# Second mixer: odd token tiles kept in opposite order of 8-token blocks, so that two token tiles share one stationary operand

## The chip, the core and the metric

The kernel runs on one core of a Trainium2 chip. The time is that of one execution on the device, in microseconds (us). The kernel before takes 2377.02 us, the median of three runs (2376.27 to 2377.44). It is written engine by engine: each of the five engines (TensorE, VectorE, ScalarE, GpSimd and SyncE, which issues most DMAs) works through its own list in order, and semaphores order them among each other.

## The reference

Four layers over 512 tokens of width 1024, in fp32, each a mixer and a feed-forward network. The change is in the second mixer, a gated recurrence with 8 heads of width 128. For each head:

```python
f = lb + (1.0 - lb) * jax.nn.sigmoid(f_logit)      # forget gate, per token and key channel
k = 1.0 - f
b = cumsum(log(f))                                 # along the tokens
o_inter = einsum('bhtk,bhkv->bhtv', q_t * exp(b_t), state)
decay = exp(where(causal, b_t - b_s, -inf))        # t: query token, s: key token
scores = einsum('bhtk,bhsk,bhtsk->bhts', q_t, k_t, decay)
o = o_inter + einsum('bhts,bhsv->bhtv', scores, v_t)
new_state = exp(b_last)[..., None] * state + einsum('bhsk,bhsv->bhkv', k_t * exp(b_last - b_t), v_t)
# then rmsnorm(o, g_norm_w) * silu(g), and a projection with w_out
```

## The kernel before

The 512 tokens are four tiles of 128. The recurrence is computed with a state for each tile, and the scores within a tile need exp(b_t - b_s) for each pair of tokens. That factor can't be split into a query and a key factor over the whole tile without overflow, so the tile is cut in four **levels** and a rest. Level 0 takes queries of the second 64 tokens against keys of the first 64; level 1 does the same within each block of 64 (32 against 32), level 2 within 32, level 3 within 16; **near** is what is left, inside blocks of 8. At level l the middle value of b in each block is subtracted from both sides: queries get exp(b - middle), keys exp(middle - b).

The tile `lv[l]` (128 channels by 512 tokens) holds, at level l, key factors in the first half of each block and query factors in the second. GpSimd writes the exponents (L1984 queries, L1985 keys, 256 columns each, for levels 1 to 3; level 0 is done by ScalarE from b itself, L1668 and L1673). ScalarE takes exp in place (`ex`, L1646), VectorE multiplies with q and k (L1848, and L1822 in the helper `tt_`). TensorE then multiplies, for each token tile, the whole 128 columns of `lv[l]` as the stationary operand with the 64 query columns as the moving one (`level`, L1521): 4 matmuls a level, 16 a head, of 128 by 64 results. All of them are fp32, and each appears in the profile as two passes. VectorE's `take` (L1836) copies the valid parts of the results into the score tile under a mask, ScalarE does it for level 0 (`taken`). Near has its own tiles `near_q` and `near_k` and 128 columns for both (L1530).

The loop runs in **rounds** p = 0 to 10, and each engine has its own order of a round. In round p head p is projected (two units of weights: q, then the forget logits), head m = p-1 has its levels, head b = p-2 its near products, state and output, head o = p-3 its norm. What closes the round is a chain over all engines:

- TensorE ends the second unit of head p (bank 1). VectorE reads it (L1939, writes `sq`), ScalarE makes four activations of it, VectorE makes k (L1947) and the scan that gives b (L1952; its semaphore is `hg_b`).
- With b, GpSimd runs through levels 1, 2, 3 (semaphore `hg_d` after each) and then near (L1988), which waits until TensorE has read the old `near_q`. ScalarE runs through level 0, level 1, the state's query factor, a weight conversion, levels 2 and 3 (waiting on `hg_d`), the copy of q out of bank 0, then `factor_log` (L1679: reads the norm's sum from bank 4), exp, the copy `keys`, near and the decayed keys.
- TensorE, meanwhile, does levels 0 and 1 of head m, the output of head b, levels 2 and 3, the first unit of the next round, `norm`, `near` and `turn`. `turn` (L1498, four transposes into bank 4) waits for `hg_rstd`, that is for ScalarE's `factor_log`, which reads the same bank. Behind it stand the second unit of that round and the state products.

Heads 0 to 7 get their b at 720.92, 736.02, 753.09, 771.60, 790.36, 809.33, 828.41 and 847.50 us. I call "+x" a time x us after the b of a head. After the last head TensorE fills the remaining waits with parts of the output projection (`part`).

## Time and profile before

| | us |
|---|---|
| median of three runs | 2377.02 |
| profiled execution | 2377.56 |
| its span, first to last instruction | 2375.8 |
| TensorE busy | 2364.9 (100%) |
| VectorE busy | 1326.7 (56%) |
| ScalarE busy | 1031.4 (43%) |
| GpSimd busy | 62.4 (3%) |
| chain of waits | TensorE 95%, VectorE 3%, ScalarE 2% |

Between the span and the profiled execution's time lie 1.8 us, outside of all instructions. The profile names engines PE (TensorE), PEld (its weight loads), DVE (VectorE), ACT (ScalarE), POOL (GpSimd) and SP. A matmul's duration holds its way through the array, so matmuls overlap: the time that a group costs is its busy time over its count, not its mean duration. The heads of the second mixer lie between 716 and 883 us.

### The profile page before, as it was taken

The page shows a single profiled execution, that of the slowest core. Times are in us where ns is not written, and L with a number is a line of the kernel's source. Part 1 is how long each engine was busy: PE and PEld are TensorE (multiplying, and loading weights), DVE is VectorE, ACT ScalarE, POOL GpSimd, SP SyncE. Part 2 cuts the span into 40 slices and gives each one's busy share as a digit, 9 for nine tenths or more (in the row PEclk, how much of TensorE's full clock was granted, in tenths as well). Part 3 has the DMA queues.
Part 4 walks back from the last instruction along what each step waited for, and adds up shares of the span by engine and source line. Part 5 has one row for each costly group of instructions (what it writes and reads, how often), then busy time and mean ns, then how long its engine had stood idle before and what let it go on. Part 6 is the DMA issues. An engine that isn't in the chain of part 4 may idle for free.

```text
span 2375.8 us, 30572 instructions
## 1 busy us (share of the span) xinstructions
PE 2364.9 (100%) x11344; PEld 1946.5 (82%) x11344; DVE 1326.7 (56%) x1950; ACT 1031.4 (43%) x1655; POOL 62.4 (3%) x100
## 2 busy tenths in 40 slices
PE   9999999999999999999999999999999999999999
PEld 7777888888888888888888778888888878888887
DVE  6765744432637867444325776777533556677731
ACT  5555522222447855222324664444322545444420
POOL 1000000000002310000000000000001000000000
PEclk9999999999999999999999999999999999999999
DMA  4112222332221113323322113232323222222332
GB/s 159 54 63 80 89 89 90 105 122 91 81 98 63 54 54 98 97 88 101 116 94 89 63 45 116 89 103 92 107 97 107 80 71 96 92 96 95 104 98 83
DMA packets 69332, 214.30 MB, mean 90 GB/s; under 512 B 7280, under 2 KB 18544, under 8 KB 69232
## 3 DMA queue, kind: packets, MB, share of 16 engines
q1 hardware_dynamic: 67696, 210.72, 26.8%
q0 software_dynamic: 1536, 2.21, 0.3%
q8 instruction: 67, 1.10, 0.2%
q14 instruction: 33, 0.27, 0.0%
HBM read 210.80 MB, written 2.10 MB: 90 GB/s over the span
## 4 chain that ended last, share of the span: by engine, by line
PE 95%; DVE 3%; ACT 2%; issue 0%; DMA 0%; SPq 0%; DVEq 0%; ACTq 0%
PE bank L264 26%; PE bank L266 26%; PE bank L265 26%; PE bank L387 5%; PE bank L379 4%; PE bank L1134 1%; PE bank L1521 1%; PE bank L1125 1%; PE bank L1171 1%; PE bank L2061 0%; DVE w_lo L238 0%; DMA raw<-in_w_fox_v 0%; PE bank L2509 0%; PE bank L2497 0%; DVE h L612 0%
## 5 line engine op out<-in xcount | busy, mean ns | idle before, releaser
L264 PE MATMUL bank<-x_hi,w_hi 128*128 128x512 f32 x1792 | 706.9, 394 | 0.1
L266 PE MATMUL bank<-x_hi,w_lo 128*128 128x512 f32 x1792 | 698.5, 390 | 0.0
L265 PE MATMUL bank<-x_lo,w_hi 128*128 128x512 f32 x1792 | 698.3, 390 | 0.0
L238 DVE TENSOR_TENSOR w_lo<-raw,w_hi 128x1024 fp32r<-128x1024 f32 (+1 forms) x367 | 470.4, 1291 | 239.8 <-ACT w_hi L233 239.0
L233 ACT ACTIVATE w_hi<-raw 128x1024 fp32r<-128x1024 f32 (+1 forms) x367 | 403.7, 1109 | 170.7 <-PE bank L266 102.7
L264 PEld LDWEIGHTS bank<-x_hi,w_hi 128*128 128x128 f32 x1792 | 336.7, 188 | 74.1 <-issue 4.2
L266 PEld LDWEIGHTS bank<-x_hi,w_lo 128*128 128x128 f32 x1792 | 336.8, 188 | 70.9
L265 PEld LDWEIGHTS bank<-x_lo,w_hi 128*128 128x128 f32 x1792 | 336.8, 188 | 70.3 <-issue 1.9
L920 DVE TENSOR_TENSOR bank<-bank,rstd 128x512 f32<-128x512 f32 x176 | 122.6, 699 | 292.9 <-PE bank L266 291.8
L264 PE MATMUL bank<-up_a_hi,w_hi 128*128 128x512 f32 (+1 forms) x748 | 282.0, 377 | 0.0
L266 PE MATMUL bank<-up_a_hi,w_lo 128*128 128x512 f32 (+1 forms) x748 | 281.6, 377 | 0.0
L265 PE MATMUL bank<-up_a_lo,w_hi 128*128 128x512 f32 (+1 forms) x748 | 281.6, 377 | 0.0
L264 PEld LDWEIGHTS bank<-up_a_hi,w_hi 128*128 128x128 f32 x748 | 140.7, 188 | 25.9
L265 PEld LDWEIGHTS bank<-up_a_lo,w_hi 128*128 128x128 f32 x748 | 140.7, 188 | 25.8
L266 PEld LDWEIGHTS bank<-up_a_hi,w_lo 128*128 128x128 f32 x748 | 140.7, 188 | 25.7
L886 ACT ACTIVATE up_a_hi<-gated 128x512 f32 (+1 forms) x88 | 55.6, 632 | 222.4 <-DVE gated L956 222.1
L734 DVE TENSOR_TENSOR h<-h,bank 128x512 f32<-128x512 f32 x32 | 22.0, 686 | 152.0 <-PE bank L266 152.0
L264 PE MATMUL bank<-mix_hi,w_hi 128*128 128x512 f32 (+1 forms) x272 | 106.1, 390 | 0.5 <-ACT y L720 0.5
L266 PE MATMUL bank<-mix_hi,w_lo 128*128 128x512 f32 (+1 forms) x272 | 102.6, 377 | 0.0
L265 PE MATMUL bank<-mix_lo,w_hi 128*128 128x512 f32 (+1 forms) x272 | 102.6, 377 | 0.0
L877 ACT ACTIVATE up_conv_g<-bank,cols 128x512 f32<-128x512 f32 x44 | 34.3, 779 | 139.7 <-DVE bank L920 139.7
L379 PE MATMUL bank<-w_hi,x_hi 128*128 128x512 f32 x224 | 88.7, 398 | 1.4 <-DVE x_lo L504 1.2
(361 smaller groups left out, 2714.8 us busy)
## 6 DMA issues: line engine op xcount, KB each, us to landing
raw<-in_w_up SPq DMA_DIRECT2D x176, 512.0 KB, 3.3
raw<-in_w_down SPq DMA_DIRECT2D x64, 704.0 KB, 4.4
raw<-in_w_fox_qk SPq DMA_DIRECT2D x16, 512.0 KB, 3.3
raw<-in_w_hgrn_qf SPq DMA_DIRECT2D x16, 512.0 KB, 3.3
raw<-in_w_fox_out SPq DMA_DIRECT2D x8, 512.0 KB, 3.2
raw<-in_w_hgrn_v SPq DMA_DIRECT2D x8, 512.0 KB, 3.4
raw<-in_w_hgrn_g SPq DMA_DIRECT2D x8, 512.0 KB, 3.2
raw<-in_w_hgrn_out SPq DMA_DIRECT2D x8, 512.0 KB, 3.3
```

Source lines behind the costliest of these rows:

```text
L233: nc.scalar.activation(w_hi[:, slot, 0:size], raw[:, slot % 2, 0:size], ACT.Copy).then_inc(sem("hi_ready"), 1)
L238: nc.vector.tensor_tensor(w_lo[:, slot, 0:size], raw[:, slot % 2, 0:size], w_hi[:, slot, 0:size].bitcast(F32), ALU.subtract).then_inc(sem( ...
L264: nc.tensor.matmul(out, w[0], x[0], start=first, stop=False)
L265: nc.tensor.matmul(out, w[0], x[1], start=False, stop=False)
L266: return nc.tensor.matmul(out, w[1], x[0], start=False, stop=last)
L379: return nc.tensor.matmul(ps[bank + tt][:].rearrange("p (n x) -> p n x", n=2), (x_hi, x_lo)[x_part][:, k, tt * P:(tt + 1) * P], w, start=f ...
L387: return nc.tensor.matmul(ps[bank + n][:, half], (w_hi, w_lo)[w_part][:, k // 2, at:at + P], (x_hi, x_lo)[x_part][:, k, half], start=first ...
L877: nc.scalar.activation(buf, ps[up_bank(j, 2 * p + half)][:], ACT.Identity, bias=cols[:, bass.ds(cb + 6 * FT + idx, 1)], scale=cols[:, bass ...
L886: nc.scalar.activation(a_hi[:, ft, :], gated[:, p, :], ACT.Copy).then_inc(sem("ahi_ready"), 1)
L920: nc.vector.tensor_tensor(bank[:], bank[:], rstd[:], ALU.mult).then_inc(sem("scaled"), 1)
L1125: ins = nc.tensor.transpose(ps[bank][:, at:at + P], prob[:, src:src + P], ident[:])
L1134: ins = nc.tensor.matmul(ps[bank][r, kt * P:T], v[:, kt, r], pt[hd][:, PT_AT[kt]:PT_AT[kt] + n], start=kt == 0, stop=kt == TT - 1)
```

## The change

Each `lv[l]` now holds keys in its left 256 columns (`lv_k`) and queries in its right 256 (`lv_q`), without gaps. The token tiles are taken in pairs (0, 1) and (2, 3). The even tile of a pair keeps its order, and its keys lie in the first halves of the blocks; the odd tile's blocks of 8 tokens are kept in opposite order, so that its keys lie in the second halves. So 128 columns hold the 64 keys of both tiles. One matmul has these as stationary operand and the 64 queries of each of the two tiles, 128 columns, as moving one.

What follows from that layout: `hk`, `near_k` and `kd_flat` hold even tiles first, then the odd ones with their blocks reversed; the masks are built for even and odd tiles; the value tiles of odd token tiles are written to `hv_odd` (in the place that `hq` and `hk` take later) and moved into `hv` by 16 DMAs with their 8-row blocks reversed; TensorE waits for these (`hg_turned`) before the heads.

```diff
+        hv_odd = nc.alloc_sbuf_tensor_at("hgrn_v_odd", [P, 8, 2, P], F32, offset=hg.at)
-        hk = [hg.take(f"k_{x}", [P, T]) for x in "ab"]
+        hk = [hg.take(f"k_{x}", [P, 2, 2, P]) for x in "ab"]
+        lv_k, lv_q = [t[:, 0:T // 2] for t in lv], [t[:, T // 2:T] for t in lv]
...
+        def in_order(t, odd):
+            return eights(t)[:, :, ::-1, :] if odd else eights(t)
...
+            wait(pe, "hg_turned", 16 * 16)
             def level(m, l):
...
-                for tt in range(TT):
-                    t = lv[l][:, tt * P:(tt + 1) * P]
-                    at = 256 * (l % 2) + 64 * tt
-                    out = ps[2 + l // 2][:, at:at + 64].rearrange("p (g y) -> p g y", y=64 >> l)
-                    ins = nc.tensor.matmul(out, t, halves(t, l)[:, :, 1, :], start=True, stop=True)
+                for u in range(2):
+                    sl = slice(u * P, (u + 1) * P)
+                    at = 256 * (l % 2) + P * u
+                    ins = nc.tensor.matmul(ps[2 + l // 2][:, at:at + P], lv_k[l][:, sl], lv_q[l][:, sl], start=True, stop=True)
...
+                            to = lv_k[0][:, P * (tt // 2) + 64 * (tt % 2):P * (tt // 2) + 64 * (tt % 2) + 64]
+                            nc.scalar.activation(row(to, tt % 2), row(hb[:, tt * P:mid + 1], 0), ACT.Exp,
...
-                        ex(near_k[:], near_q[:], "hg_e", -1.0)
+                        for odd in range(2):
+                            ins = nc.scalar.activation(in_order(near_k[:, odd], odd), eights(parity(near_q[:], odd)), ACT.Exp, scale=-1.0)
+                        ins.then_inc(sem("hg_e"), 1)
...
-                        cp(halves(scs[m % 2][:], 0)[0:64, :, 1, :], ps[2][0:64, 0:256].rearrange("p (g y) -> p g y", y=64),
-                           "hg_take0")
+                        for odd in range(2):
+                            r = ROWS[odd]
+                            ins = nc.scalar.activation(parity(scs[m % 2][:], odd)[r, :, 64:P],
+                                                       ps[2][r, 0:256].rearrange("p (u o y) -> p u o y", u=2, o=2)[:, :, odd, :], ACT.Copy)
+                        ins.then_inc(sem("hg_take0"), 1)
...
-            dve.wait_ge(sem("hg_consts"), 32)
+            dve.wait_ge(sem("hg_consts"), 16 * 18)
+            wait(dve, "hg_masks", 8)
...
-                        t = halves(lv[l][:], l)
-                        nc.vector.tensor_tensor(t[:, :, 1, :], halves(hq[m % 2][:], l)[:, :, 1, :], t[:, :, 1, :], ALU.mult)
-                        tt_(t[:, :, 0, :], halves(hk[m % 2][:], l)[:, :, 0, :], t[:, :, 0, :], ALU.mult, "hg_pr")
+                        q = packed(lv_q[l], l)
+                        nc.vector.tensor_tensor(q, halves(hq[m % 2][:], l)[:, :, 1, :], q, ALU.mult)
+                        k = lv_k[l].rearrange("p (g x y) -> p g x y", x=2, y=64 >> l)
+                        tt_(k, keys_of(hk[m % 2], l), k, ALU.mult, "hg_pr")
...
-                    nc.vector.tensor_scalar(hk[p % 2][:], sg1, lbt[:, 8, p:p + 1], lbt[:, 7, p:p + 1],
-                                            ALU.mult, ALU.add).then_inc(sem("hg_k"), 1)
+                    for odd in range(2):
+                        ins = nc.vector.tensor_scalar(in_order(hk[p % 2][:, odd], odd), eights(parity(sg1, odd)), lbt[:, 8, p:p + 1],
+                                                      lbt[:, 7, p:p + 1], ALU.mult, ALU.add)
+                    ins.then_inc(sem("hg_k"), 1)
...
+            for a in range(0, P, 8):
+                nc.gpsimd.dma_start(raw_masks[1][P - 8 - a:P - a], io["lv_mask"][a:a + 8]).then_inc(sem("hg_consts"), 16)
             nc.gpsimd.dma_start(scan_mask[:], io["scan_mask"]).then_inc(sem("hg_consts"), 16)
+            wait(pool, "hg_consts", 16 * 18)
+            pool.wait_ge(sem("tokens_out"), 16)
+            for a in range(0, P, 8):
+                to = hv[P - 8 - a:P - a].rearrange("p m (u o) c -> p (m u) o c", o=2)[:, :, 1, :]
+                nc.gpsimd.dma_start(to, hv_odd[a:a + 8].rearrange("p m u c -> p (m u) c")).then_inc(sem("hg_turned"), 16)
...
-                    nc.gpsimd.tensor_tensor(d_[:, :, 1, :], b_[:, :, 1, :], middle, ALU.subtract)
-                    nc.gpsimd.tensor_tensor(d_[:, :, 0, :], middle, b_[:, :, 0, :], ALU.subtract).then_inc(sem("hg_d"), 1)
+                    nc.gpsimd.tensor_tensor(packed(lv_q[l], l), b_[:, :, 1, :], middle, ALU.subtract)
+                    even = hb[:].rearrange("p (u o g x y) -> p u o g x y", u=2, o=2, x=2, y=half)[:, :, 0, :, 0, :]
+                    nc.gpsimd.tensor_tensor(by_role(lv_k[l], l)[:, :, :, 0, :],
+                                            even[:, :, :, half - 1:half].to_broadcast([P, 2, 64 // half, half]), even, ALU.subtract)
+                    for u in range(2):
+                        odd = halves(hb[:, P * (2 * u + 1):P * (2 * u + 2)], l)[:, :, 0, :]
+                        to = eights(halves(lv_k[l][:, P * u:P * (u + 1)], l)[:, :, 1, :])[:, ::-1, ::-1, :]
+                        ins = nc.gpsimd.tensor_tensor(to, eights(odd[:, :, half - 1:half].to_broadcast([P, 64 // half, half])),
+                                                      eights(odd), ALU.subtract)
+                    ins.then_inc(sem("hg_d"), 1)
```

TensorE, the levels and the output of one round, first before, then changed (line numbers are each kernel's own; `hgrn_lv_108` to `111` before and `109` to `112` after are the tiles of levels 0 to 3):

```order
L1521 MATMUL bank<-hgrn_lv_108 128x64 x4
L1521 MATMUL bank<-hgrn_lv_109 128x64 x4
L1557 MATMUL bank<-hgrn_scores_b,hgrn_v 128x128 x2
L1559 MATMUL bank<-hgrn_qe_b,hgrn_st 128x128
...
L1521 MATMUL bank<-hgrn_lv_110 128x64 x4
L1521 MATMUL bank<-hgrn_lv_111 128x64 x4
```

```order
L1557 MATMUL bank<-hgrn_lv_109 128x128 x2
L1557 MATMUL bank<-hgrn_lv_110 128x128 x2
L1595 MATMUL bank<-hgrn_scores_b,hgrn_v 128x128 x2
L1597 MATMUL bank<-hgrn_qe_b,hgrn_st 128x128
...
L1557 MATMUL bank<-hgrn_lv_111 128x128 x2
L1557 MATMUL bank<-hgrn_lv_112 128x128 x2
```

Nothing has moved; each level is two matmuls of 128 columns where it was four of 64.

GpSimd, one head, before and changed (`hgrn_b` is the scan's result, the tiles of levels 1 to 3 are `109` to `111` before and `110` to `112` after):

```order
L1984 TENSOR_TENSOR hgrn_lv_109<-hgrn_b 128x8x32
L1985 TENSOR_TENSOR hgrn_lv_109<-hgrn_b 128x8x32
L1984 TENSOR_TENSOR hgrn_lv_110<-hgrn_b 128x16x16
L1985 TENSOR_TENSOR hgrn_lv_110<-hgrn_b 128x16x16
L1984 TENSOR_TENSOR hgrn_lv_111<-hgrn_b 128x32x8
L1985 TENSOR_TENSOR hgrn_lv_111<-hgrn_b 128x32x8
L1988 TENSOR_TENSOR hgrn_near_q<-hgrn_b 128x512
```

```order
L2049 TENSOR_TENSOR hgrn_lv_110<-hgrn_b 128x4x32
L2054 TENSOR_TENSOR hgrn_lv_110<-hgrn_b 128x2x4x8 x2
L2047 TENSOR_TENSOR hgrn_lv_111<-hgrn_b 128x256
L2049 TENSOR_TENSOR hgrn_lv_111<-hgrn_b 128x8x16
L2054 TENSOR_TENSOR hgrn_lv_111<-hgrn_b 128x4x2x8 x2
L2047 TENSOR_TENSOR hgrn_lv_112<-hgrn_b 128x256
L2049 TENSOR_TENSOR hgrn_lv_112<-hgrn_b 128x16x8
L2054 TENSOR_TENSOR hgrn_lv_112<-hgrn_b 128x8x8 x2
L2059 TENSOR_TENSOR hgrn_near_q<-hgrn_b 128x512
```

The queries' instruction stays (L2047, of 256 columns; that of the first level stands just above the piece), and the keys' one of 256 has become three: one of 128 columns and two of 64. A head has 12 level instructions on GpSimd where it had 6.

## Rows read from the trace of the kernel before

**Rows 1.** Busy time by engine, heads 3 to 6 (stretch, us, then engines, PEclk, DMA)
```profile
771.60:847.50 75.90, 75.90 (x456) 65.83 (x455) 61.99 (x108) 60.56 (x132) 20.48 (x29) 1.00 0.17 56
```

**Rows 2.** TensorE's levels among its groups: shape, count | busy us, mean ns | idle
```profile
L1521 PE MATMUL bank<-hgrn_lv 128*128 128x64 f32 x256 | 30.4, 272 | 0.0
```

**Rows 3.** Chain of waits, round of head 6 (start us, us, what)
```profile
823.51 1.73 PE bank L1521 x16
...
834.99 0.89 PE bank L1530 x8
835.88 0.51 PE bank L1498 x4
...
842.60 1.73 PE bank L1521 x16
```

**Rows 4.** TensorE's waits, whole program
```profile
PE bank L1498 <- ACT hgrn_hr L1679: 1.9, 1, 1.9
```

**Rows 5.** Chain of waits, turn of head 1 and what follows
```profile
757.88 0.63 PE bank L1498 x4
...
766.27 1.73 PE bank L1521 x16
```

**Rows 6.** Busy time, TensorE's clock just behind that wait
```profile
760.00:761.00 1.00, 1.00 (x3) 0.72 (x3) 1.00 (x2) 0.97 (x3) 0.00 (x0) 0.50 0.00 0
```

**Rows 7.** GpSimd in order of time (start us, us, instruction)
```profile
616.04 0.58 POOL L1976 DMA_DIRECT2D hgrn_lv_mask<-in_lv_mask  x1 [607.01 <-PE bank L266]
...
720.92 0.63 POOL L1984 TENSOR_TENSOR hgrn_lv<-hgrn_b 128x256 f32<-128x256 f32 x1 [103.77 <-DVE hgrn_b L1952]
...
771.60 0.63 POOL L1984 TENSOR_TENSOR hgrn_lv<-hgrn_b 128x256 f32<-128x256 f32 x1 [13.38 <-DVE hgrn_b L1952]
...
828.41 0.64 POOL L1984 TENSOR_TENSOR hgrn_lv<-hgrn_b 128x256 f32<-128x256 f32 x1 [10.49 <-DVE hgrn_b L1952]
...
830.76 0.86 POOL L1984 TENSOR_TENSOR hgrn_lv<-hgrn_b 128x256 f32<-128x256 f32 x1
831.58 0.80 POOL L1985 TENSOR_TENSOR hgrn_lv<-hgrn_b 128x256 f32<-128x256 f32 x1
835.97 1.04 POOL L1988 TENSOR_TENSOR hgrn_near_q<-hgrn_b 128x512 f32<-128x512 f32 x1 [3.59 <-PE bank L1530]
847.50 0.63 POOL L1984 TENSOR_TENSOR hgrn_lv<-hgrn_b 128x256 f32<-128x256 f32 x1 [10.49 <-DVE hgrn_b L1952]
```

**Rows 8.** VectorE in order of time, head 6 and the last head
```profile
823.55 0.69 DVE L1939 TENSOR_SCALAR sq<-bank 128x512 f32<-128x512 f32 x1 [0.20 <-PE bank L266]
...
830.62 0.46 DVE L1848 TENSOR_TENSOR hgrn_lv<-hgrn_q_a,hgrn_lv 128x256 f32<-128x256 f32 x1 [1.07 <-ACT hgrn_lv L1673]
831.00 0.90 DVE L1822 TENSOR_TENSOR hgrn_lv<-hgrn_k_a,hgrn_lv 128x256 f32<-128x256 f32 x1
...
832.58 0.41 DVE L1822 TENSOR_TENSOR hgrn_lv<-hgrn_k_a,hgrn_lv 128x256 f32<-128x256 f32 x1
...
838.37 0.69 DVE L1822 TENSOR_TENSOR hgrn_near_k<-hgrn_k_a,hgrn_near_k 128x512 f32<-128x512 f32 x1 [1.01 <-ACT hgrn_near_q L1646]
...
842.63 0.69 DVE L1939 TENSOR_SCALAR sq<-bank 128x512 f32<-128x512 f32 x1 [0.20 <-PE bank L266]
...
859.99 0.69 DVE L1822 TENSOR_TENSOR hgrn_near_q<-hgrn_q_b,hgrn_near_q 128x512 f32<-128x512 f32 x1
```

**Rows 9.** TensorE in order of time, the last head's near products
```profile
862.47 1.06 PE L1530 MATMUL bank<-hgrn_near_q,hgrn_near_k 128*128 128x128 f32 x8
```

**Rows 10.** ScalarE in order of time, head 6
```profile
832.48 1.14 ACT L1646 ACTIVATE hgrn_lv<-hgrn_lv 128x512 f32<-128x512 f32 x2
...
835.03 0.60 ACT L1679 ACTIVATE hgrn_hr<-bank 128x512 f32<-128x512 f32 x1 [0.26 <-PE bank L1566]
```

**Rows 11.** ScalarE in order of time, entry: last value tiles
```profile
662.96 2.41 ACT L583 ACTIVATE hgrn_v<-bank,cols 128x512 f32<-128x512 f32 x4
```

**Rows 12.** VectorE in order of time, before the heads
```profile
702.48 0.06 DVE L1818 MEMSET hgrn_scan_mask<- 128x4 f32 x1
```

More of the change, by code:

```diff
@@ L1479, in build @@
         st = hg.take("st", [P, TT - 1, P])
-        lv_mask = hg.take("lv_mask", [P, 4, P], U32)
+        lv_mask = [hg.take(f"lv_mask{l}", [P, T // 2], U32) for l in range(1, LEVELS)]
+        near_mask = hg.take("near_mask", [P, 2, P], U32)
         scan_mask = hg.take("scan_mask", [P, T])
@@ L1529, in near @@
                     sl = slice(tt * P, (tt + 1) * P)
-                    ins = nc.tensor.matmul(ps[6][:, sl], near_k[:, sl], near_q[:, sl], start=True, stop=True)
+                    ins = nc.tensor.matmul(ps[6][:, sl], near_k[:, tt % 2, tt // 2, :], near_q[:, sl], start=True, stop=True)
                 ins.then_inc(sem("hg_lv"), 1)
@@ L1637, in act_hgrn @@
         def act_hgrn(act):
[L1639 removed]
+            act_enter(act, 2, lambda b, tt: hv_odd[:, 4 * b:4 * b + 4, tt // 2, :] if tt % 2 else hv[:, 4 * b:4 * b + 4, tt, :])
             act.wait_ge(sem("hg_lb"), 1)
@@ L1730, in decayed @@
                             last = (tt + 1) * P - 1
-                            ins = nc.scalar.activation(kd_flat[:, sl], hb[:, sl], ACT.Exp, bias=hb[:, last:last + 1], scale=-1.0)
+                            to = kd_flat[:, tt % 2, tt // 2, :]
+                            ins = nc.scalar.activation(row(to, tt % 2), row(hb[:, sl], 0), ACT.Exp, bias=hb[:, last:last + 1],
+                                                       scale=-1.0)
                         ins.then_inc(sem("hg_e"), 1)
```

53 lines of the change are left out of this document (38 added, 15 removed).

## The prediction

> **What bounds the kernel now.** I read the page first: TensorE is busy for the whole span. The busy time by stretch then shows that this holds in the changed stage as well, from head 3 to head 7: 75.90 of 75.90 us [rows 1]. So time that TensorE is spared there is time gained, as long as nothing else stands right behind it. But VectorE (61.99) and ScalarE (60.56) are busy for four fifths of the same stretch [rows 1], in one chain with each other, and the question is how much slack they have.
>
> The chain of waits gives a round: levels at 823.51, the same at 842.60, so 19.09 us [rows 3]. GpSimd's first instruction of a head marks when b is there: heads 0, 3, 6 and 7 at 720.92, 771.60, 828.41 and 847.50 [rows 7]. The last round took 19.09 us and the four from head 3 on 75.90 together, while the three before took 50.68. In those first rounds VectorE sets the pace, TensorE runs ahead and is idle once, 1.9 us at the turn that waits for ScalarE [rows 4]. That wait is the place to watch: in round 6 ScalarE's log (L1679) ends at 835.63 [rows 10] and the turn starts at 835.88 [rows 3]. The slack is a semaphore's way long.
>
> **What TensorE saves.** Its level group is 256 passes, busy 30.4 us [rows 2], part of it overlap at the ends; the chain has 16 of them in 1.73 us, 108 ns each [rows 3]. The nearest row for 128 columns is near: 8 passes in 0.89 us, 111 ns each [rows 3]. So the columns are nearly free and the passes cost. The change makes 16 passes of a head's 32: 32 x 108 - 16 x 111 = 3.46 - 1.78 = 1.7 us a head, 13.5 us in all. If the wider matmul cost twice as much, it would be nothing; the near row speaks against that. A round of TensorE's work falls from 19.09 to 17.4.
>
> **What the other engines pay in a round.** Per level GpSimd has one instruction of 256 columns, one of 128 and two of 64 in place of two of 256. A 256 one takes 0.64 alone and a 512 one 1.04 [rows 7]: 1.6 ns a column and 0.2 fixed, from start to start about 0.6, 0.37 and 0.27 for 256, 128 and 64. A level takes 1.5 instead of 1.2, three levels 1.0 more. That is an estimate by extrapolation, and blocks that are walked backwards are in no row. Bounds: nothing (if an instruction costs by its columns alone) and 2.5 us a head (if a backward one of 64 costs as much as one of 128 and a little more). I take 1.0.
>
> There is a second cost, since GpSimd and VectorE hinder each other. VectorE's product with 256 columns takes 0.41 when GpSimd is idle (832.58) and 0.90 at 831.00; the latter ends 0.28 after GpSimd's instruction of 830.76 does (831.62), and GpSimd's next one, started at 831.58, needs 0.80 for what takes 0.6 [rows 7, 8]. So each waits for the other's running instruction, one by one in turn. I lay out the new head by that. GpSimd is at level 2's keys when VectorE starts its products at +2.2 (830.62 [rows 8]), and has seven level instructions left where it had three. They alternate with VectorE's products: the last key instruction of level 3 ends at about +5.9, in place of +3.97 (832.38) [rows 7].
>
> ScalarE takes up levels 2 and 3 at +4.07 and needs 1.14 for both [rows 10]. Level 3 would start at +6.0, not +4.6, and end at +6.6. The copy of q and the log follow, 0.5 apart and 0.6 long as the log's row shows: log done at +7.7. The turn starts at +7.8, and from the turn to the next round's levels TensorE needs 842.60 - 835.88 = 6.72 us [rows 3]: +14.5. VectorE reads bank 1 at once (0.03 after the levels' row, 842.63), b follows 828.41 - 823.55 = 4.86 later [rows 7, 8], and the split of k in two adds 0.1 (fixed part of one more instruction). That closes the round at **19.6 us**.
>
> VectorE's own chain gives the same. From its first product (830.62) to bank 1 (842.63) lie 12.0 us, with 1.0 of idle time ahead of 838.37, 0.2 ahead of bank 1, and about 1.0 lost to GpSimd [rows 8]. The rest is 9.8. Now near_q's exponents come earlier as TensorE is faster, and GpSimd's instruction of 1.04 [rows 7] then meets VectorE's conversion instead of its reads of PSUM; the loss becomes some 2.7. So 4.86 + 2.2 + 9.8 + 2.7 = 19.6. Two chains of equal length make the number firmer.
>
> **What the wait does to the clock.** TensorE's work of 17.4 in a round of 19.6 leaves a wait of 2.2 us at each turn. The one wait of that size in the trace, 1.9 us ahead of the turn at 757.88, is followed by a stretch at a granted clock of 0.50, the 1.2 GHz level [rows 4, 6]; from that turn to the next levels it took 766.27 - 757.88 = 8.39 us where round 6 took 6.72 [rows 3, 5]. So such a wait costs 1.67 more, and it lies in the chain that closes the round. A round with it takes 21.3. Bounds: in no round and in each; I take it in 6 of 10, 1.0 us a round.
>
> **The sum**, against the profiled execution (2377.56; the median is 0.5 below):
> - Heads 0 to 3: VectorE sets the pace, and what TensorE saves is idle time. VectorE loses 0.6 more to GpSimd and 0.1 in k: 3 x 0.7 = +2.1. Bounds 0 and +6.
> - Heads 3 to 7: 4 x (19.6 + 1.0) - 75.90 = +6.5. Bounds: 4 x 18.4 - 75.90 = -2.3 (no loss to GpSimd's longer list) and 4 x 21.3 - 75.90 = +9.3.
> - Behind head 7's b: the levels of heads 6 and 7 are 3.4 us shorter, and TensorE has parts of the output projection to fill with. But the last head's products are not far ahead: near_q is there at 860.68 for a matmul at 862.47 [rows 8, 9], 1.8 us. ScalarE's start into that head comes earlier with TensorE's norm, which gives some of it back. I take -2.2, bounds -3.4 and 0.
> - ScalarE's near in two instructions and `taken` in two: 0.2 each (the fixed part). Taken lies in ScalarE's wait for b; near stands in front of VectorE's near products, which are as late for VectorE's own sake. Nothing, or 0.2 a round.
> - The turning of the values: the last value tiles are written at 665.4 [rows 11], 16 issues of 0.58 [rows 7] end at 675 and 14 small copies at about 680. VectorE gets to its wait at 702 [rows 12], TensorE later still. Hidden, with more than 20 us to go; if it weren't, each us late is one lost. The 17 mask DMAs go out from 616 on and have longer.
>
> 2.1 + 6.5 - 2.2 = +6.4: 2384.0, or 2383.5 on the scale of the median.
>
> The Trainium skill has a price for GpSimd's small instructions ("GPSIMD Engine Reference", section 3.1, Elementwise): about 2.6 cycles an element for two inputs, at 1.2 GHz. Set against the 0.6 us of a 256-column one it leaves almost no fixed part, a level would grow by an estimated 0.1 us instead of 0.3, level 3 would come before +5.3, and the round would end near 19.0 us, as long as today's; the slope between this trace's rows of 256 and 512 columns is 1.6 ns, not 2.2, so the trace doesn't agree, and no row shows 64 columns. It would bring the time toward the second rival below.
>
> **Rivals.**
> - TensorE stays the bound and gets all of it: -13.5, so 2363.5. For it: it is busy without a gap now [rows 1]. Against it: the log reaches the turn with 0.25 us to spare, and the chain over VectorE can't close in 17.4. Chance 0.05.
> - Faster, by one mechanism: GpSimd's split instructions cost by columns alone, so level 3's exponents are at hand when ScalarE comes for them. The round is then 4.86 to b, +5.2 end of level 3, +6.4 log, +6.5 turn, +13.2 bank 1: with VectorE's own length about 18.4. Heads 3 to 7 give -2.3, the tail -2.2, the first heads nothing: 2372.5. It decides at the point where level 3's `hg_d` comes before +4.6. Chance 0.10.
> - The round is 19.6, but a wait of 2.2 us leaves the clock alone (one example is thin): 2.1 + 2.5 - 2.2 = +2.4, 2379.5. Chance 0.22.
> - Backward blocks are slow on GpSimd, 0.2 more for each of six instructions: 1.2 us more in each of seven rounds, +8 on top: 2391.5. For it: no row shows them. Chance 0.13.
> - The forecast, 2383.5, with its own range of 2380 to 2388: chance 0.50.
>
> About 0.2%, 4.8 us, is what a measurement of this kernel can tell from no change. Faster by that: the first rival and half of the second, 0.11. Within: the third, the rest of the second and a fifth of the forecast, 0.34. Slower: 0.55. The range goes from the second rival to the fourth, 2372 to 2392.
>
> **What would show it.** Right: L1557's passes number 128 at about 111 ns; TensorE waits at nearly each turn for ScalarE's log, some 2 us; the busy time by stretch has a granted clock of 0.5 for some 3 us behind more than half of these waits; b is 20 to 21 us apart from head 3 on; GpSimd's 64-column instructions take 0.3. Wrong: turns without waits and rounds below 19 us (then level 3's exponents came in time), waits without a fall of the clock, or a wait on `hg_turned` or the masks before the heads.

## The result, and the profile after

| | before | changed |
|---|---|---|
| median, us (9 runs each) | 2377.4 (2376.27 to 2379.15) | 2384.62 (2382.88 to 2386.37) |
| profiled execution; span | 2377.56; 2375.8 | 2383.5; 2381.7 |
| TensorE, GpSimd busy | 2364.9, 62.4 | 2355.5, 98.0 |
| b of heads 0, 3, 7 at | 720.92, 771.60, 847.50 | 720.92, 771.97, 852.41 |

The changed kernel is slower: ratio 1.0029, 95% interval 1.0021 to 1.0038. Of the 5.9 us between the two profiled executions 0.4 arise in heads 0 to 3, 4.5 in heads 3 to 7, and 1.0 behind head 7's b.

TensorE saved what it should. The group of its levels, from the costliest groups of the changed kernel (busy us, mean ns of one | idle time ahead, and what ended it), answers to [rows 2]: half the passes, 17.4 us busy where it was 30.4.

```profile
L1557 PE MATMUL bank<-hgrn_lv 128*128 128x128 f32 x128 | 17.4, 277 | 2.0 <-DVE hgrn_lv L1869 2.0
```

And it lost more than that in waits: its busy time fell by 9.4 us in all and the span grew by 5.9, so it is idle for 15.3 us more. Its two largest waits over the whole program (us, times, longest); before, the one at the turn was 1.9 us [rows 4]:

```profile
PE bank L1575 <- ACT hgrn_hr L1718: 11.3, 6, 2.8
PE bank L1595 <- DVE hgrn_st L1944: 2.8, 4, 1.1
```

The busy time by stretch (us, then PE, PEld, DVE, ACT, POOL busy, PEclk, DMA) answers to [rows 1] and [rows 6]. From head 3 to head 7 TensorE is busy for 70.58 of 80.44 us; the rest it waits. The three single microseconds lie behind three turns that waited, and only the last two stand at a granted clock of 0.50:

```profile
771.97:852.41 80.44, 70.58 (x383) 59.40 (x382) 67.09 (x113) 61.14 (x140) 27.97 (x52) 0.96 0.16 53
781.00:782.00 1.00, 1.00 (x6) 0.83 (x5) 1.00 (x2) 0.97 (x3) 0.00 (x0) 1.00 0.76 188
...
820.00:821.00 1.00, 1.00 (x4) 0.81 (x3) 0.86 (x3) 0.97 (x4) 0.00 (x0) 0.50 0.67 254
840.00:841.00 1.00, 1.00 (x4) 0.80 (x3) 1.00 (x3) 0.97 (x3) 0.00 (x0) 0.50 0.38 74
```

Five turns waited for 1.9 us or more. Four of them follow in TensorE's order of time; the fifth is at 798.89, with 1.91. Behind 757.97, 779.56 and 798.89 the clock stayed at 1.00, behind 818.21 and 839.10 it fell to half for 3 to 4 us, after a shorter wait than the first two:

```profile
757.97 0.63 PE L1575 MATMUL bank<-ident,hgrn_kd_flat 128*128 128x128 f32 x4 [2.21 <-ACT hgrn_hr L1718]
...
779.56 0.63 PE L1575 MATMUL bank<-ident,hgrn_kd_flat 128*128 128x128 f32 x4 [2.78 <-ACT hgrn_hr L1718]
...
818.21 0.63 PE L1575 MATMUL bank<-ident,hgrn_kd_flat 128*128 128x128 f32 x4 [1.92 <-ACT hgrn_hr L1718]
...
839.10 0.63 PE L1575 MATMUL bank<-ident,hgrn_kd_flat 128*128 128x128 f32 x4 [1.91 <-ACT hgrn_hr L1718]
```

What the turn waits for starts on GpSimd. Its order of time answers to [rows 7]; head 4 stands for all. The 64-column instructions are two of 0.27 from start to start when it is alone (792.25) and 0.6 each when VectorE is at its products (795.94); level 3 ends at 797.11, 5.8 us behind b:

```profile
771.97 0.63 POOL L2047 TENSOR_TENSOR hgrn_lv<-hgrn_b 128x256 f32<-128x256 f32 x1 [11.79 <-DVE hgrn_b L2000]
...
791.30 0.63 POOL L2047 TENSOR_TENSOR hgrn_lv<-hgrn_b 128x256 f32<-128x256 f32 x1 [12.34 <-DVE hgrn_b L2000]
791.89 0.40 POOL L2049 TENSOR_TENSOR hgrn_lv<-hgrn_b 128x128 f32<-128x128 f32 x1
792.25 0.54 POOL L2054 TENSOR_TENSOR hgrn_lv<-hgrn_b 128x64 f32<-128x64 f32 x2
...
795.94 1.17 POOL L2054 TENSOR_TENSOR hgrn_lv<-hgrn_b 128x64 f32<-128x64 f32 x2
797.07 1.22 POOL L2059 TENSOR_TENSOR hgrn_near_q<-hgrn_b 128x512 f32<-128x512 f32 x1
810.61 0.64 POOL L2047 TENSOR_TENSOR hgrn_lv<-hgrn_b 128x256 f32<-128x256 f32 x1 [12.32 <-DVE hgrn_b L2000]
...
831.50 0.63 POOL L2047 TENSOR_TENSOR hgrn_lv<-hgrn_b 128x256 f32<-128x256 f32 x1 [13.89 <-DVE hgrn_b L2000]
...
852.41 0.63 POOL L2047 TENSOR_TENSOR hgrn_lv<-hgrn_b 128x256 f32<-128x256 f32 x1 [13.91 <-DVE hgrn_b L2000]
```

ScalarE's level 3 waits 1.16 us for it and the log comes after, for [rows 10]:

```profile
797.14 0.63 ACT L1684 ACTIVATE hgrn_lv<-hgrn_lv 128x512 f32<-128x512 f32 x1 [1.16 <-POOL hgrn_lv L2054]
...
798.16 0.59 ACT L1718 ACTIVATE hgrn_hr<-bank 128x512 f32<-128x512 f32 x1
```

VectorE in the same head, for [rows 8]: products of 0.51 and 0.89, a conversion of 2.06 us (near_q's exponents at 797.07 lie across it; before it took 1.22), and the clamp of the logits (the read of bank 1) 12.2 us behind the first product. The last product ends with the copy under the near mask at 799.96:

```profile
793.51 0.53 DVE L1893 TENSOR_TENSOR hgrn_lv<-hgrn_q_a,hgrn_lv 128x256 f32<-128x256 f32 x1 [1.48 <-ACT hgrn_lv L1712]
...
794.83 0.89 DVE L1869 TENSOR_TENSOR hgrn_lv<-hgrn_k_a,hgrn_lv 128x256 f32<-128x256 f32 x1
...
797.31 2.06 DVE L238 TENSOR_TENSOR w_lo<-raw,w_hi 128x1024 fp32r<-128x1024 f32 x1
...
799.96 0.74 DVE L1878 COPY_PREDICATED hgrn_scores_b<-hgrn_near_mask,bank 128x512 f32<-128x512 uint32 x1
...
805.74 0.69 DVE L1985 TENSOR_SCALAR sq<-bank 128x512 f32<-128x512 f32 x1 [0.22 <-PE bank L266]
```

Behind head 7's b the chain of waits no longer runs along TensorE, as it did before, but through VectorE's list for the last head (start us, us, what):

```profile
867.95 1.22 DVE w_lo L238
...
872.60 0.70 DVE hgrn_ho L1869
...
874.92 0.36 DVE hgrn_st L1944
...
879.09 0.86 PE bank L1604 x2
```

The last norm's first matmul starts at 878.92 where before it was 873.52.

### The profile page after: what moved, and what is told of

Read it like the earlier page. It is cut to its first block, busy times and chain, and to the rows that moved or that the text cites. A ratio compares the mean times of both kernels' runs of the same rounds, so it can differ in the third digit from the quotient of the medians.

```text
span 2381.7 us, 30437 instructions
## 1 busy us (share of the span) xinstructions
PE 2355.5 (99%) x11216; PEld 1934.6 (81%) x11216; DVE 1334.0 (56%) x1958; ACT 1034.5 (43%) x1671; POOL 98.0 (4%) x194
## 4 chain that ended last, share of the span: by engine, by line
PE 89%; DVE 5%; ACT 3%; POOL 1%; issue 1%; DMA 1%; DVEq 0%; ACTq 0%; SPq 0%
PE bank L264 25%; PE bank L266 25%; PE bank L265 25%; PE bank L387 5%; PE bank L379 4%; PE bank L1134 1%; PE bank L1125 1%; PE bank L1171 1%; DVE w_lo L238 1%; PE bank L2132 0%; ACT sq L1684 0%; POOL hgrn_lv L2054 0%; DVE hgrn_b L2000 0%; DMA raw<-in_w_up 0%; POOL hgrn_lv L2047 0%
## 5 line engine op out<-in xcount | busy, mean ns | idle before, releaser
L238 DVE TENSOR_TENSOR w_lo<-raw,w_hi 128x1024 fp32r<-128x1024 f32 (+1 forms) x367 | 476.3, 1307 | 239.4 <-ACT w_hi L233 238.5
L264 PEld LDWEIGHTS bank<-up_a_hi,w_hi 128*128 128x128 f32 x748 | 140.7, 188 | 25.8
L266 PEld LDWEIGHTS bank<-up_a_hi,w_lo 128*128 128x128 f32 x748 | 140.7, 188 | 25.6
L877 ACT ACTIVATE up_conv_g<-bank,cols 128x512 f32<-128x512 f32 x44 | 34.3, 779 | 139.7 <-DVE bank L920 139.7
```

Source lines behind the costliest of these rows:

```text
L238: nc.vector.tensor_tensor(w_lo[:, slot, 0:size], raw[:, slot % 2, 0:size], w_hi[:, slot, 0:size].bitcast(F32), ALU.subtract).then_inc(sem( ...
L264: nc.tensor.matmul(out, w[0], x[0], start=first, stop=False)
L266: return nc.tensor.matmul(out, w[1], x[0], start=False, stop=last)
L877: nc.scalar.activation(buf, ps[up_bank(j, 2 * p + half)][:], ACT.Identity, bias=cols[:, bass.ds(cb + 6 * FT + idx, 1)], scale=cols[:, bass ...
```

## The experiments

Twelve kernels, each timed against the kernel before on the same chip. The times of the kernel before were 2377.60 to 2377.66 in each set. A round is the distance of b from head 3 to head 7 over four; the waits are TensorE's at the turns; the last column counts the turns and norms with a wait of 1.88 us or more, and how many of them had a stretch at half clock behind them. All but the times are read from one profile each. The letters (T, A to G, L) name the theories and rivals of the expectation that is printed with each experiment. The 95% intervals are some 2 us wide to either side; where two experiments differ by less, the reading rests on the rounds of the profiles, which repeat from head to head, and not on the medians.

| kernel | us | ratio (95%) | b 0, 3, 7 | round | waits at turns | half clock |
|---|---|---|---|---|---|---|
| before | 2377.6 | 1 | 720.92, 771.60, 847.50 | 18.98 | 1.9 | 1 of 1 |
| changed | 2384.62 | 1.0029 (1.0021–1.0038) | 720.92, 771.97, 852.41 | 20.11 | 11.3 | 2 of 5 |
| 1 TensorE's part alone | 2375.37 | 0.999 (0.9981–0.9999) | 720.87, 771.16, 845.30 | 18.54 | 6.9 | 1 of 1 |
| 2 all but TensorE's part | 2380.36 | 1.0013 (1.0004–1.0022) | 721.30, 772.48, 849.77 | 19.32 | 3.8 | 0 of 2 |
| 3 GpSimd's list short | 2375.69 | 0.9991 (0.9982–1.0) | 720.54, 770.83, 844.98 | 18.54 | 7.2 | 1 of 1 |
| 4 filled waits | 2379.86 | 1.0009 (1.0–1.0018) | 720.56, 771.66, 848.75 | 19.27 | 1.8 | none |
| 5 log first | 2377.81 | 1.0001 (0.9992–1.001) | 720.59, 771.65, 846.74 | 18.77 | 6.8 | 0 of 2 |
| 6 b turned once | 2378.95 | 1.0006 (0.9997–1.0015) | 721.16, 772.68, 848.50 | 18.96 | 8.8 | 0 of 2 |
| 7 both | 2378.89 | 1.0006 (0.9997–1.0015) | 720.55, 772.06, 847.91 | 18.96 | 6.5 | 1 of 2 |
| 8 both, first state on ScalarE | 2377.39 | 0.9999 (0.999–1.0008) | 720.49, 771.67, 846.15 | 18.62 | 6.5 | 1 of 2 |
| 9 log first, first state on ScalarE | 2376.36 | 0.9994 (0.9985–1.0003) | 721.65, 772.38, 846.17 | 18.45 | 6.2 | 1 of 2 |
| 10 the same, low half on GpSimd | 2373.32 | 0.9982 (0.9973–0.9991) | 721.03, 771.15, 842.73 | 17.90 | 4.6 | 0 of 1 |
| 11 kernel before, with the edits of 9 | 2376.8 | 0.9999 (0.999–1.0008) | 721.21, 771.55, 846.34 | 18.70 | 1.9 | 0 of 1 |
| 12 one more GpSimd instruction | 2383.97 | 1.0027 (1.0017–1.0037) | 721.04, 774.61, 853.12 | 19.63 | 6.7 | 1 of 2 |

**1. TensorE's part alone**, in the kernel before:

```diff
-                for tt in range(TT):
-                    t = lv[l][:, tt * P:(tt + 1) * P]
-                    at = 256 * (l % 2) + 64 * tt
+                for u in range(2):
+                    t = lv[l][:, 2 * u * P:(2 * u + 1) * P]
+                    at = 256 * (l % 2) + P * u
...
+                    two = lv[l][:, 2 * u * P:(2 * u + 2) * P]
+                    ins = nc.tensor.matmul(out, t, halves(two, l)[:, :, 1, :], start=True, stop=True)
```

> The kernel before, in which TensorE alone is changed: each level is two matmuls of 128 columns (the key operand of an even token tile for both tiles of the pair) in place of four of 64. GpSimd, ScalarE and VectorE run their old lists; the scores of the odd tiles come out wrong. Theory T (what TensorE saves turns into waits because the round over VectorE, GpSimd, ScalarE's log and the turn is nearly as long): b comes every 18.4 to 18.8 us from head 3 on instead of 19.0, TensorE waits 1 to 1.5 us at the turns for ScalarE's log, total 2372 to 2376, so at most a third of the 13.5 us that the passes save. Rival A (TensorE is the bound and the loss in the changed kernel comes from the other engines' longer lists alone): rounds of 17.4, total 2363.5. Rival B (128-column passes bring nothing): 2377.

Measured 2375.37, rounds of 18.54: theory T. Of 13.5 us on TensorE 2.3 reach the end; the rest stands in its waits (6.9 us at the turns, where it was 1.9).

It also isolates the tail: b of head 7 comes 2.2 us sooner than before and the profiled execution ends 2.3 sooner, so behind head 7 the shorter levels bring nothing, or 0.1.

**2. All but TensorE's part:** the changed kernel with four matmuls of 64 columns a level.

```diff
-                for u in range(2):
-                    sl = slice(u * P, (u + 1) * P)
+                for tt in range(TT):
+                    keys = lv_k[l][:, (tt // 2) * P:(tt // 2 + 1) * P]
...
+                    ins = nc.tensor.matmul(ps[2 + l // 2][:, at:at + 64], keys, lv_q[l][:, 64 * tt:64 * tt + 64], start=True, stop=True)
```

> The changed kernel, in which TensorE still takes four matmuls of 64 columns a level (the shared key operand is loaded for each tile); everything else as in the changed kernel. Theory T: the round is closed by the other engines, so TensorE's extra 1.7 us a head fall into its waits: rounds of 19.3 with waits at the turns of 0.2 to 0.5 us and the granted clock never at half behind them, except early; total 2381 to 2385, the same as the changed kernel or up to 3 us faster because the two rounds at half clock go. Rival A (TensorE's time counts): 1.7 us a head more, 2384.6 + 8 or more = 2392 to 2398.

Measured 2380.36, rounds of 19.32 as in the undisturbed ones of the changed kernel (19.33 and 19.31). TensorE has 1.7 us a head more to do and the kernel is 4.3 us faster than the changed one, more than T's 3 (the time is 0.6 under T's range): of the changed kernel's waits the last three before the tail are gone (798.89, 818.21 and 839.10), and with them the stretches at half clock. Two are left:

```profile
PE bank L1575 <- ACT hgrn_hr L1718: 3.8, 2, 1.9
```

**3. GpSimd's list short:**

```diff
-                    nc.gpsimd.tensor_tensor(by_role(lv_k[l], l)[:, :, :, 0, :],
...
-                    for u in range(2):
...
+                    nc.gpsimd.tensor_tensor(packed(lv_k[l], l), middle, b_[:, :, 0, :], ALU.subtract).then_inc(sem("hg_d"), 1)
```

> The changed kernel, in which GpSimd writes a level's key exponents with one instruction of 256 columns, in natural order, where the changed kernel has one of 128 and two of 64 (the scores of the odd tiles come out wrong). Theory T (GpSimd's longer list makes level 3 late and holds VectorE up): level 3's exponents come at +4.0 to +4.3 after b instead of +5.8, ScalarE doesn't wait for them, rounds 18.4 to 18.8, total 2372 to 2376. Rival C (the loss is from the turning, the split instructions of ScalarE and VectorE, or the clock): 2382 to 2385, rounds unchanged at 19.3 and more.

Measured 2375.69 and 18.54: T, and within 0.3 us of experiment 1, which has none of the other edits. So the turning of values and masks, the two-part instructions of ScalarE and VectorE and the reversed blocks there cost nothing that shows; GpSimd's list makes the whole 0.78 us a round (19.32 against 18.54). GpSimd ends level 3 at 830.39, 3.95 behind b, and VectorE has no idle time between its first product and the clamp, 11.5 us later (GpSimd, then VectorE, in order of time):

```profile
829.60 0.79 POOL L2048 TENSOR_TENSOR hgrn_lv<-hgrn_b 128x256 f32<-128x256 f32 x1
831.70 1.15 POOL L2051 TENSOR_TENSOR hgrn_near_q<-hgrn_b 128x512 f32<-128x512 f32 x1 [1.30 <-PE bank L1566]
```

```profile
828.65 0.46 DVE L1893 TENSOR_TENSOR hgrn_lv<-hgrn_q_a,hgrn_lv 128x256 f32<-128x256 f32 x1 [1.48 <-ACT hgrn_lv L1712]
...
840.13 0.69 DVE L1985 TENSOR_SCALAR sq<-bank 128x512 f32<-128x512 f32 x1
```

**4. Filled waits:**

```diff
                 wait(pe, "hg_kdh", m)
+                if 1 <= m <= 5:
+                    wait(pe, "hg_st", 3 * m)
+                    for _ in range(8):
+                        nc.tensor.matmul(ps[5][:, 0:P], ones[:], ident[:], start=True, stop=True)
                 wait(pe, "hg_rstd", 2 * norms - 1)
```

> The changed kernel with eight extra TensorE matmuls of 128 columns (constants into a bank that is free then) ahead of the wait for ScalarE's log at the turns of heads 1 to 5, so that TensorE is busy for about 1.8 us where it waited 1.9 to 2.8. Theory D (a part of the loss is the clock: two rounds of 20.9 among those of 19.3): no stretch at half clock from head 3 on, all rounds 19.3, total 2381 to 2382, 3 us under the changed kernel. Rival E (the longer rounds have another cause and the clock follows): 2384.6 as the changed kernel. If the eight matmuls take more than the wait: 2386 to 2390.

Measured 2379.86, rounds of 19.27, no stretch at half clock: theory D, with 4.8 us back where 3 were expected (its range began at 2381). Between the two profiled executions it is 4.2, of which 3.4 from head 3 to head 7, two stretches of 1.6 and a little. The rest may lie in the choice of the profiled execution. The changed kernel's nine executions had mean granted clocks of 0.997 to 0.999, three of each: those at 0.999 (the profiled one among them) took 2383.6 on average, those at 0.998 2384.2, those at 0.997 2385.3. The filled kernel's had 1.000 each and lie within 0.8 us. So by and large the executions with more time at half clock are the longer ones. The waits for the log are down to 1.8 us, the longest to 0.9.

**5. Log first,** in the changed kernel, on ScalarE:

```diff
-                        if o:
+                        if o and p >= HEADS:
                             factor_log()
...
                     level(2)
-                    level(3)
                     used(act, u0 + 2 * p)
                     wait(act, "hg_qe", p - 1)
                     cp(hq[p % 2][:], ps[0][:], "hg_q")
+                    if norm and o:
+                        factor_log()
+                    level(3)
                     factor()
```

> The changed kernel with ScalarE's order altered in heads 1 to 4 and on: behind level 2's exponents it takes the copy of q and the norm's log first and level 3's exponents after them, so the turn no longer waits behind GpSimd's list. Two theories of what closes the 19.3 us round. Theory F (two chains of equal length, the log's over TensorE and VectorE's own list with what it loses to GpSimd): the turns come 1 us or more sooner, VectorE loses its 0.2 and 0.1 us of idle time, rounds of 18.9 to 19.1, no stretch at half clock from head 3 on, total 2378.5 to 2381. Theory G (the log's chain alone closes it, VectorE only follows): rounds of 17.8 to 18.3, total 2372 to 2376.

Measured 2377.81, rounds of 18.77: neither range, but near F's (0.1 us a round and 0.7 in the time under it) and 0.5 a round above G's. The turn comes sooner, with 1.02 us of waiting, and VectorE has no idle time from its first product to the clamp, 11.7 us in place of 12.2 (VectorE, then TensorE):

```profile
811.40 0.53 DVE L1895 TENSOR_TENSOR hgrn_lv<-hgrn_q_b,hgrn_lv 128x256 f32<-128x256 f32 x1 [1.48 <-ACT hgrn_lv L1712]
...
815.21 2.06 DVE L238 TENSOR_TENSOR w_lo<-raw,w_hi 128x1024 fp32r<-128x1024 f32 x1
817.19 0.41 DVE L1895 TENSOR_TENSOR hgrn_lv<-hgrn_q_b,hgrn_lv 128x256 f32<-128x256 f32 x1
...
817.86 0.72 DVE L1880 COPY_PREDICATED hgrn_scores_a<-hgrn_near_mask,bank 128x512 f32<-128x512 uint32 x1
...
823.10 0.69 DVE L1987 TENSOR_SCALAR sq<-bank 128x512 f32<-128x512 f32 x1
```

```profile
814.99 0.63 PE L1575 MATMUL bank<-ident,hgrn_kd_flat 128*128 128x128 f32 x4 [1.02 <-ACT hgrn_hr L1718]
```

So the log's chain closed the changed kernel's round, and VectorE's list stood 0.55 us behind it. Of the 0.78 us a round that GpSimd's longer list costs (experiment 3), 0.55 went through level 3, the log and the turn; 0.23 (18.77 against 18.54) is what it takes from VectorE.

**6. b turned once:** VectorE copies b behind the scan, and GpSimd needs two instructions of 256 columns a level.

```diff
+                    wait(pool, "hg_bt", m + 1)
+                    k = lv_k[l].rearrange("p (g x y) -> p g x y", x=2, y=half)
+                    nc.gpsimd.tensor_tensor(k, middles_of(hbt, l), keys_of(hbt, l), ALU.subtract).then_inc(sem("hg_d"), 1)
...
+                    for odd in range(2):
+                        ins = nc.vector.tensor_copy(in_order(hbt[:, odd], odd), eights(parity(hb[:], odd)))
```

> The changed kernel with full output: VectorE copies b once per head behind the scan, odd tiles in the opposite order of blocks, and GpSimd then needs one instruction of 256 columns for a level's keys instead of 128 + 64 + 64. VectorE has 1.5 us of idle time behind the scan for the two copies (some 0.7 us). Theory T (GpSimd's list is what costs): level 3's exponents at +4.3 to +4.8, rounds of 18.5 to 18.8, total 2374.5 to 2377, under the kernel before by 1 to 3 us. Rival (the copies wait for GpSimd's lock and push the first products or level 1 back by 0.5 us): rounds of 19.0, 2378 to 2379.

Measured 2378.95, rounds of 18.96: the rival, though level 3's exponents are there at +4.4, as T had it. The two engines meet at the copy, GpSimd's first key instruction starts at +0.97 where it was +0.6, and VectorE's first three products (0.87, 0.89 and 0.83) each meet one of GpSimd's instructions; the product of the queries takes 1.55 us, since near_q's exponents lie across it (GpSimd, then VectorE):

```profile
829.54 0.74 POOL L2058 TENSOR_TENSOR hgrn_lv<-hgrn_b 128x256 f32<-128x256 f32 x1 [12.46 <-DVE hgrn_b L2007]
830.51 0.62 POOL L2061 TENSOR_TENSOR hgrn_lv<-hgrn_b_turned 128x256 f32<-128x256 f32 x1 [0.23 <-DVE hgrn_b_turned L2010]
```

```profile
831.75 0.87 DVE L1900 TENSOR_TENSOR hgrn_lv<-hgrn_q_a,hgrn_lv 128x256 f32<-128x256 f32 x1 [0.50 <-ACT hgrn_lv L1719]
...
834.44 1.55 DVE L1876 TENSOR_TENSOR hgrn_qe_a<-hgrn_q_a,hgrn_qe_a 128x512 f32<-128x512 f32 x1
```

**7. Both edits.**

> The two edits together: b copied in turned order for GpSimd, and ScalarE's log ahead of level 3. Theory F (VectorE's list closes the round once GpSimd's is short: no idle time on it from the first product to the clamp of the logits): rounds of 18.4 to 18.6 as without the log's edit, total 2373.5 to 2376.5, with TensorE's waits moved from the turn to the norm or the levels. Theory G (the log at the turn closes it): rounds of 17.4 to 17.8, total 2368 to 2371.

Measured 2378.89, rounds of 18.96, the same as 6 to 0.01 us, though TensorE's waits at the turns fell from 8.8 to 6.5 us. Both ranges were missed. G is out by 1.2 us a round: the log at the turn isn't the bound once VectorE's list is longer. F's mechanism may stand, but its figures were too low, since they rested on those expected for experiment 6.

**8. The first state on ScalarE,** added to 7:

```diff
+                def first_state():
+                    wait(act, "hg_ds", b + 1)
+                    wait(act, "hg_o", b)
+                    cp(st[:, 0, :], ps[5][:, 0:P], "hg_st")
...
-                        nc.vector.tensor_copy(st[:, 0, :], ps[5][:, 0:P]).then_inc(sem("hg_st"), 1)
+                        if not (proj and b > 0):
+                            nc.vector.tensor_copy(st[:, 0, :], ps[5][:, 0:P]).then_inc(sem("hg_st"), 1)
```

> The same two edits and a third: ScalarE, idle there for 1.6 us, makes the first state copy of heads 1 to 5 (128 columns from PSUM, 0.29 to 0.33 us on VectorE) in VectorE's place. Theory F (VectorE's list is the bound): each round 0.3 shorter than with the two edits, 18.1 to 18.3, total 1.0 to 2.0 us less than with the two. Theory G or any other bound (TensorE, ScalarE): no difference.

Measured 2377.39: 1.5 us less than 7, the round 0.34 less, for an instruction of 0.3 on VectorE. That is F, on its mechanism; the absolute 18.1 to 18.3 missed with 7.

**9. The same edit on experiment 5.**

> The changed kernel with two edits of ScalarE's order, and nothing on GpSimd: the norm's log ahead of level 3 (18.78 us a round, 2377.8, alone), and the first state copy of heads 1 to 5 on ScalarE in VectorE's place. Theory F (VectorE's list, without idle time from the first product to the clamp, closes the round): the copy's 0.30 to 0.33 us comes off each round, 18.45 us, total 2375.3 to 2376.3, under the kernel before. Rival (another engine is as long by now): 18.7 and more, 2377.2 to 2378.

Measured 2376.36 and 18.45. F, at the edge: the round is as expected to 0.01, the time 0.1 above the range.

**10. The low half on GpSimd,** added to 9:

```diff
+                if 0 <= m - 2 < HEADS - 3:
+                    wait(pool, "hg_outh", m - 1)
+                    nc.gpsimd.tensor_tensor(mix_lo[:, m - 2, :], ho, mix_hi[:, m - 2, :].bitcast(F32),
+                                            ALU.subtract).then_inc(sem("hg_out"), 1)
```

> As the kernel above, and GpSimd, idle for 10 us of each round, subtracts the low half of the mixed output (512 columns) for heads 0 to 4 in VectorE's place. VectorE's instruction is 0.60 us long, GpSimd's 1.04, and VectorE's neighbours there that read PSUM (the states, the clamp) don't collide with it. Theory F with collisions: between nothing and 0.4 us less a round, 18.05 to 18.45, total 2373 to 2376. If the whole of GpSimd's instruction falls on VectorE's SBUF-only instructions: 0.4 us more a round, 2378.

Measured 2373.32, 11.3 us under the changed kernel and 4.3 under the one before; its interval doesn't reach 1. The round fell by 0.55, to 17.90, which is nearly all of VectorE's 0.60 and 0.15 more than the most that was expected. GpSimd's instruction lies beside VectorE's states and clamp, which read PSUM, and these keep their 0.73 and 0.69 (GpSimd, then VectorE):

```profile
819.43 1.28 POOL L2073 TENSOR_TENSOR mix_lo<-hgrn_ho,mix_hi 128x512 fp32r<-128x512 f32 x1 [5.58 <-ACT mix_hi L1687]
```

```profile
819.20 0.73 DVE L1954 SCALAR_TENSOR_TENSOR hgrn_st<-hgrn_st,hgrn_dec_a,bank 128x128 f32<-128x128 f32 x2
820.01 0.69 DVE L1995 TENSOR_SCALAR sq<-bank 128x512 f32<-128x512 f32 x1
```

**11. The edits of 9 on the kernel before.**

> The kernel before with the same two edits of ScalarE's order (the log ahead of level 3, the first state copy on ScalarE). Theory T (the kernel before is bound by TensorE from head 3 on, the changed one by VectorE): rounds of 19.0 to 19.09 as before, total 2375.5 to 2377.6 (the only gain at head 1's turn, whose wait and clock cost at most 2 us). Rival (VectorE or the log bound the kernel before too): rounds of 18.7, 2374 or less.

Measured 2376.8: within T's range, no difference from before. The mean round is the rival's, though: 18.19 and 18.41 at first, then 19.11 and 19.08. VectorE still set the pace in those first rounds, which T had not said; relieved, it seems to let TensorE use up its lead, until TensorE is the bound again (GpSimd's first instruction of heads 4 to 6):

```profile
789.74 0.63 POOL L1994 TENSOR_TENSOR hgrn_lv<-hgrn_b 128x256 f32<-128x256 f32 x1 [10.32 <-DVE hgrn_b L1962]
...
808.15 0.63 POOL L1994 TENSOR_TENSOR hgrn_lv<-hgrn_b 128x256 f32<-128x256 f32 x1 [10.48 <-DVE hgrn_b L1962]
...
827.26 0.64 POOL L1994 TENSOR_TENSOR hgrn_lv<-hgrn_b 128x256 f32<-128x256 f32 x1 [10.50 <-DVE hgrn_b L1962]
```

Its executions fall into two groups: seven with a mean granted clock of 1.000 took 2376.1 to 2377.0 us, four with 0.999 took 2378.2 to 2379.2.

So the relief of VectorE in 9 is worth nothing that can be measured in the kernel before, TensorE's part alone 2.3 us, and the changed kernel with the further relief of 10 4.3. That further relief wasn't tried on the kernel before; its rounds of 17.90 are shorter than the 19.09 that TensorE needs there.

**12. One more GpSimd instruction,** on experiment 5's kernel:

```diff
+                if m < HEADS - 1:
+                    nc.gpsimd.tensor_tensor(unused[:], scan_mask[:], scan_mask[:], ALU.subtract).then_inc(sem("hg_unused"), 1)
```

> The changed kernel with the log ahead of level 3 (18.78 us a round, 2377.8, alone), and one more GpSimd instruction a head, 512 columns, 1.04 us, behind near_q's exponents, with sources nobody writes and an output nobody reads. No engine waits for it and GpSimd has 10 us of idle time behind it, so it can only cost by holding VectorE up. Theory L (VectorE and GpSimd take turns instruction by instruction, and VectorE's list is the bound): VectorE's level 3 products wait for it, rounds of 19.5 to 19.8, total 2382 to 2385. Rival (GpSimd's load is free where nobody waits for its result): 18.8 and 2377.8.

Measured 2383.97, rounds of 19.63: L. Nobody waits for the instruction, and it costs 6.2 us. It stretches VectorE's first product of level 3 from 0.41 (817.19 in experiment 5) to 1.26, 0.85 us, and the round grew by 0.86. It itself takes 2.02, since it starts while the conversion runs; near_q's instruction, also of 512 columns, takes 1.04 alone (GpSimd, then VectorE):

```profile
819.65 1.22 POOL L2063 TENSOR_TENSOR hgrn_near_q<-hgrn_b 128x512 f32<-128x512 f32 x1
820.83 2.02 POOL L2066 TENSOR_TENSOR hgrn_unused<-hgrn_scan_mask 128x512 f32<-128x512 f32 x1
```

```profile
819.89 2.06 DVE L238 TENSOR_TENSOR w_lo<-raw,w_hi 128x1024 fp32r<-128x1024 f32 x1
821.87 1.26 DVE L1896 TENSOR_TENSOR hgrn_lv<-hgrn_q_b,hgrn_lv 128x256 f32<-128x256 f32 x1
```

## Why the prediction was right, and where it wasn't

The time was right to 1.1 us of the median, and so was its sign, but the sum is closer than its terms: two were too high (by 1.7 and 2.0) and one too low (by 3.2). That they nearly cancel is luck.

- **What TensorE saves.** Right: the group fell by 13.0 us, for 13.5 forecast. That nearly all turns into waits was right too, and experiment 1 shows it without the other edits.
- **GpSimd's list.** Right: 64 columns in 0.27, no more for blocks walked backwards, level 3 done at +5.8 for +5.9 forecast, ScalarE's wait of 1.16, the log done at +7.5 for +7.7. Experiment 3 shows that this list is the whole cost of the rest of the change, experiment 5 that it costs 0.55 us a round through the log and 0.23 through VectorE.
- **The round of 19.6.** Measured 19.32. The log's chain closed it, as forecast, and was sized right to 0.2 us (its own terms, 7.8 + 6.72 + 0.03 + 4.86 + 0.1, add up to 19.5). The step that failed is "VectorE's own chain gives the same": experiment 5 puts VectorE's own round at 18.77. The term that was mis-sized is "the loss becomes some 2.7". From the first product to the copy under the near mask VectorE has eight products, the queries' product of 512 columns and the conversion. Undisturbed, from start to start, these need 8 x 0.34 + 0.60 + 1.13 = 4.45. They took 6.45 in the changed kernel's head 4 (793.51 to 799.96) and 6.46 in experiment 5 (811.40 to 817.86), so GpSimd costs VectorE 2.0 there. In the kernel before, head 4, they took 5.37, so 0.9, near the 1.0 that the prediction took off:

```profile
792.57 0.46 DVE L1848 TENSOR_TENSOR hgrn_lv<-hgrn_q_a,hgrn_lv 128x256 f32<-128x256 f32 x1 [1.19 <-ACT hgrn_lv L1673]
...
796.13 1.22 DVE L238 TENSOR_TENSOR w_lo<-raw,w_hi 128x1024 fp32r<-128x1024 f32 x1
797.26 0.42 DVE L1848 TENSOR_TENSOR hgrn_lv<-hgrn_q_a,hgrn_lv 128x256 f32<-128x256 f32 x1
...
797.94 0.74 DVE L1829 COPY_PREDICATED hgrn_scores_b<-hgrn_lv_mask,bank 128x512 f32<-128x512 uint32 x1
```

The rest of the list is 9.7 (11.7 - 2.0) for 9.8, and 4.86 + 2.2 + 9.7 + 2.0 makes 18.8. The two chains were not of equal length, so the number was not firmer for them: one closed the round, the log's, and it could be shortened.

- **The clock.** The price was right (20.9 against 19.3, so 1.6, for 1.67). It came in two of the four long waits between heads 3 and 7 (two of five in all) where 6 of 10 were forecast: 3.2 us, where 4.0 were in the sum. That is the profiled execution; by their mean clocks others had more. Experiment 4 shows the cost by taking it away.
- **Heads 0 to 3:** +2.1 forecast, +0.4 measured, inside the bounds of 0 and 6. Experiment 1 took 50.29 there, 0.4 less than before (50.68), so not all that TensorE saves was idle time. Against that the changed kernel took 51.05: its longer lists cost 0.25 a round, the same as VectorE lost in experiment 5 (0.23), where the prediction took 0.7.
- **Heads 3 to 7:** +6.5 forecast, +4.5 measured: 4 x 19.32 - 75.90 = 1.38, and 3.16 from the clock.
- **Behind head 7's b:** the term "I take -2.2" was mis-sized. It measured +1.0 in the profiled execution, outside of its bounds of -3.4 and 0. The last head's products were too near: VectorE's list for that head is the chain there, and what TensorE spares becomes wait, as experiment 1 shows (0.1 gained). About half of the +1.0 arises in that list, which GpSimd holds up here too: from head 7's b to the last norm's first matmul it takes 26.5 us (before 26.0), 26.5 to 26.7 in experiments 2, 4 and 5, and 25.6 and 25.8 in 1 and 3, where GpSimd's list is short. The other half lies in the projection behind: from VectorE's last state of head 7 (874.92) to its last sum of squares 34.5 us pass, 34.0 before, and between 33.2 and 34.3 in experiments 1 to 5 and 10, where the work there is the same. What sets this is open.
- **Hidden work.** Right: no wait on the turned values or the masks; the medians of experiments 1 and 3 differ by 0.3 us.
- **The signs and the chances.** Two of the signs of being right did not come: the clock fell behind fewer than half of the long waits, and two of the four rounds from head 3 on took 19.3, not 20 to 21. The others came. The chances of the rivals add up to 0.10 for faster, 0.37 for within and 0.53 for slower, where the prediction has 0.11, 0.34 and 0.55.

Of the rivals, the one on TensorE is refuted by experiment 1, the one on backward blocks by the rows, the faster one by level 3's time. The one that leaves the clock alone has been produced in experiment 4: 2379.86, for the 2379.5 that it gave, though with the same errors in its first and last term.
